# Attention steps in another order: values ahead of transposes on TensorE, copies between two exponentials on ScalarE

## The reference, cut to what matters

```python
s = jnp.einsum('bhqd,bhrqwd->bhqrw', q_i, k_win).astype(jnp.float32)
s = s + jnp.transpose(bias, (0, 2, 1, 3)).astype(jnp.float32)[None]
pr = jax.nn.softmax(s.reshape(B, H, GRID_W, kh * kw), axis=-1).reshape(B, H, GRID_W, kh, kw)
return jnp.einsum('bhqrw,bhrqwd->bhqd', pr.astype(v.dtype), v_win)
```

```python
o_dil = dilated_attention(q_d, k_d, v_d, positions, slopes).reshape(B, S, -1).astype(x.dtype)
o_mla = latent_attention(cq, ckv, k_rope, positions, g_cq[l], w_q_up[l], g_ckv[l], w_kv_up[l], ...)
mix = jnp.concatenate([o_dil, o_mla], axis=-1) @ w_out[l]
```

## Time and profile before

| | before |
|---|---|
| median of 3 runs | 3013.02 us (3012.51 to 3015.49) |
| the profiled execution: its time | 3010.71 us |
| its span, first to last instruction | 3008.9 us |
| PE busy | 2906.1 us (97% of the span) |
| DVE busy | 1765.0 us (59%) |
| ACT busy | 1313.7 us (44%) |

### The profile page before, as it was taken

How to read it: one execution, slowest core, us unless ns; L and a number is a source line. 1 busy time by engine, 2 the same in 40 slices (tenths; PEclk the granted TensorE clock), 3 DMA queues, 4 the chain that set the end, 5 groups by cost and what they waited for, 6 DMA issues and landing times. The chain is left out here.

```text
span 3008.9 us, 47845 instructions
## 1 busy us (share of the span) xinstructions
PE 2906.1 (97%) x20088; PEld 2310.8 (77%) x20088; DVE 1765.0 (59%) x2421; ACT 1313.7 (44%) x2015; POOL 214.7 (7%) x353
## 2 busy tenths in 40 slices
PE   8999888999999999999999999999999999999999
PEld 6756777888888786788888875688888865788887
DVE  5357775696864767487784577553333586543332
ACT  4234443442434537443334546654152556553241
POOL 0400000100000111000000212000000212000000
PEclk9999999999999999999999999999999999999999
DMA  5310001556523231365643220023222310123222
GB/s 168 98 62 3 4 3 58 147 176 226 173 86 105 78 111 65 88 203 197 188 130 102 89 86 1 30 86 102 94 96 96 96 60 2 58 85 100 95 98 84
DMA packets 224165, 287.97 MB, mean 96 GB/s; under 512 B 8031, under 2 KB 164103, under 8 KB 217808
## 3 DMA queue, kind: packets, MB, share of 16 engines
q1 hardware_dynamic: 213632, 226.32, 23.8%
q0 software_dynamic: 8448, 54.34, 5.3%
q10 hardware_dynamic: 1872, 4.26, 0.4%
HBM read 280.70 MB, written 2.10 MB: 94 GB/s over the span
## 5 line engine op out<-in xcount | busy, mean ns | idle before, releaser
L240 DVE TENSOR_TENSOR weights_operand<-weights,weights_operand 128x2048 fp32r<-128x2048 f32 x196 | 448.8, 2290 | 450.2 <-ACT weights_operand L234 439.7
L234 ACT CAST weights_operand<-weights 128x2048 fp32r<-128x2048 f32 x196 | 374.0, 1908 | 511.9 <-PE ps L248 505.4
L246 PE MATMUL ps<-ffn_h_high,weights_operand 128*128 128x512 f32 x704 | 274.5, 390 | 2.2 <-PEq L507 2.2
L248 PE MATMUL ps<-ffn_h_high,weights_operand 128*128 128x512 f32 x704 | 273.9, 389 | 0.0
L247 PE MATMUL ps<-ffn_h_low,weights_operand 128*128 128x512 f32 x704 | 273.9, 389 | 0.0
L246 PE MATMUL ps<-mlp_h_high,weights_operand 128*128 128x512 f32 x512 | 200.3, 391 | 2.5 <-DVE mlp_h_low L828 2.1
L248 PE MATMUL ps<-mlp_h_high,weights_operand 128*128 128x512 f32 x512 | 199.3, 389 | 0.0
L247 PE MATMUL ps<-mlp_h_low,weights_operand 128*128 128x512 f32 x512 | 199.2, 389 | 0.0
L246 PE MATMUL ps<-weights_operand,mlp_hid_high 128*128 128x512 f32 x512 | 199.2, 389 | 0.0
L247 PE MATMUL ps<-weights_operand,mlp_hid_high 128*128 128x512 f32 x512 | 199.2, 389 | 0.0
L248 PE MATMUL ps<-weights_operand,mlp_hid_low 128*128 128x512 f32 x512 | 199.2, 389 | 0.0
(11 more groups left out here) (582 smaller groups left out, 6171.9 us busy)
## 6 DMA issues: line engine op xcount, KB each, us to landing
mod_w<-in_w_mod POOLq DMA_DIRECT2D x48, 1024.0 KB, 5.2
weights<-in_ffn_w_up SPq DMA_DIRECT2D x88, 512.0 KB, 5.2
weights<-in_w_mlp_in SPq DMA_DIRECT2D x32, 1024.0 KB, 5.3
weights<-in_w_mlp_out SPq DMA_DIRECT2D x32, 1024.0 KB, 5.0
weights<-in_ffn_w_down SPq DMA_DIRECT2D x24, 768.0 KB, 4.4
weights<-in_mix_w_in SPq DMA_DIRECT2D x13, 1024.0 KB, 5.3
weights<-in_na_w_qkv SPq DMA_DIRECT2D x12, 1024.0 KB, 5.1
weights<-in_w_in SPq DMA_DIRECT2D x12, 1024.0 KB, 5.4
```

What stands on the lines that cost most here:

```text
L234: nc.scalar.copy(st.high[s][:], st.raw[s][:]).then_inc(st.high_done, 1)
L240: nc.vector.tensor_tensor(st.low[s][:], st.raw[s][:], st.high[s][:], ALU.subtract).then_inc(st.split_done, 1)
L246: nc.tensor.matmul(out, lh, rh, start=start, stop=False)
L248: return nc.tensor.matmul(out, ll, rh, start=False, stop=stop)
```

## The change

Two lists are written in another order; no instruction is added or taken away, and every instruction keeps its waits. On PE the spread and values of unit s-2 stand ahead of the transposes of unit s-1 instead of behind them. On ACT the two copies of unit s-1 stand between the first and the second exponential of unit s instead of ahead of both. DVE's and POOL's lists stay. All five calls are concerned.

```diff
@@ tensor
-                    if 0 <= s - 1 < N:
-                        u = s - 1
-                        for h in range(2):
-                            pe.wait_ge(U.exp, 2 * u + h + 1)
-                            if u:
-                                pe.wait_ge(U.copied, 2 * u - 1 + h)
-                            for n in range(slots):
-                                mm = nc.tensor.transpose(ps[:, 4 + h, n * P:(n + 1) * P], S[u % 2][h][:, n * P:(n + 1) * P],
-                                                         cx.ident[:])
-                            mm.then_inc(U.turned, 1)
                     if 0 <= s - 2 < N:
                         u = s - 2
                         pe.wait_ge(U.widened, u + 1)
...
                         mm.then_inc(U.out, 1)
+                    if 0 <= s - 1 < N:
+                        u = s - 1
+                        for h in range(2):
+                            pe.wait_ge(U.exp, 2 * u + h + 1)
...
+                            mm.then_inc(U.turned, 1)
@@ scalar
+                def copy(u):
+                    for h in range(2):
+                        act.wait_ge(U.turned, 2 * u + h + 1)
...
+                def exponential(s, h):
...
                 for s in range(N + 2):
+                    if s < N:
+                        exponential(s, 0)
                     if 0 <= s - 1 < N:
...
+                        copy(s - 1)
                     if s < N:
...
+                        exponential(s, 1)
```

More of the change, by code:

```diff
@@ L3047, in _ @@
                         mm.then_inc(U.out, 1)
+                    if 0 <= s - 1 < N:
+                        u = s - 1
+                        for h in range(2):
+                            pe.wait_ge(U.exp, 2 * u + h + 1)
+                            if u:
+                                pe.wait_ge(U.copied, 2 * u - 1 + h)
+                            for n in range(slots):
+                                mm = nc.tensor.transpose(ps[:, 4 + h, n * P:(n + 1) * P], S[u % 2][h][:, n * P:(n + 1) * P],
+                                                         cx.ident[:])
+                            mm.then_inc(U.turned, 1)
             @block.scalar
@@ L3052, in _ @@
                     first[0](act)
+                def copy(u):
+                    for h in range(2):
+                        act.wait_ge(U.turned, 2 * u + h + 1)
+                        if u >= 2:
+                            act.wait_ge(U.out, u - 1)
+                        nc.scalar.copy(PT[u % 2][h][:], ps[:, 4 + h, 0:width].rearrange("p (a q) -> p a q", a=slots))\
+                            .then_inc(U.copied, 1)
+                def exponential(s, h):
+                    m = M[s % 2]
+                    act.wait_ge(U.best, 2 * s + h + 1)
+                    if s >= 2:
+                        act.wait_ge(U.turned, 2 * (s - 2) + h + 1)
+                        act.wait_ge(U.inverted, s - 1)
+                    src = S[s % 2][h][:] if score_op else ps[:, bank(s, h), :]
+                    nc.scalar.activation(S[s % 2][h][:], src, ACT.Exp, scale=exp_sign, bias=m[:, 2 + h:3 + h],
+                                         accum_out=m[:, 4 + h:5 + h]).then_inc(U.exp, 1)
                 for s in range(N + 2):
+                    if s < N:
+                        exponential(s, 0)
                     if 0 <= s - 1 < N:
[L3055 to L3061, removed]
-                    if s < N:
[L3063 to L3071, removed]
+                        copy(s - 1)
+                    if s < N:
+                        exponential(s, 1)
             @block.vector
```

## The result

| | before | after |
|---|---|---|
| median | 3013.02 us (3012.51 to 3020.93, 5 runs) | 3026.53 us (3023.53 to 3030.81, 5 runs) |
| the profiled execution: its time | 3010.71 us | 3024.65 us |
| first scores of `naa` to the end of the span | 1874.0 us | 1883.9 us |

The ratio of the times is 1.0036, with a 95% interval of 1.0023 to 1.0049: slower by 10.8 us (6.9 to 14.8), while the two medians, of five runs each, lie 13.5 apart. The sign is as forecast; the median lies 1.0 above the top of the range given, and the time that the ratio gives, 3023.9, inside it.

The account below looks back on a forecast made before the run. PE was busy 97% of the span; a loop through three engines set `naa`, DVE bounded `dia`, PE `mla`. Terms 3.3 + 4.7 - 0.9 = +7.1 us on the median 3013.0 gave 3020.1, range 3014 to 3025.5.

Parts of the forecast that it names:

- the multiplication's loop: In `dia`, spread waits for the previous unit's multiplication, transposes now between: 7.00 us per two steps, 3.50 against 3.32; +4.7 both calls.
- the copies' loop: In `naa`, values wait for copies behind the first exponential: 4.43 us per two steps, 0.11 more a step, +3.3 us.
- Ends of calls: At call ends, last spread's shorter wait and last exponential's place behind two copies taken as equal: 0.
- `mla`: In `mla`, PE bounds and nothing new waits: minus 0.10 plus 0.07, -0.03 us a step; thirty steps, -0.9.
- The loops have slack: Rival for `naa` and `dia`: unseen slack in the loops, so little happens, 3012.1 us; chance 0.35.
- The waits for the exponential go and nothing takes their place: Rival: in `naa` PE does values during its 0.33 wait, step falls to 2.00; in all -9.1 us, 3003.9; chance 0.05.
- Changes of shape: On PE in `naa` and `dia`, four changes of array shape a step instead of three: 0.09 us more.

## Why the prediction came out as it did

- **`dia`, the multiplication's loop: right.** 7.00 was worked out for two steps, 7.00 measured (3.37 + 3.63), with the wait where it was looked for. Opening and steady steps give +2.3 in `dia0`, the term as predicted. That ScalarE has no part in it is shown by PE's half alone (3.50), that the spread closes it by the spread put late (3.32).
- **`naa`, the copies' loop: the size of a step right, the mechanism half the story.** 0.11 a step was predicted; 0.11 was measured over 12 steps, 0.13 over the 25 of the table (3.15 in all). But "before, the copies ... were no part" left out that the multiplication's loop, worked out for `dia` alone, also closes in `naa`: in the kernel with PE's half alone it is 0.79 from scores to score operation (1186.25), 1.57 to the multiplication (1187.82), 0.53 to the spread, 0.23 to the values, 0.59 to the transposes and 0.59 to the next scores, 4.30 for two steps. PE's order by itself so costs about 0.05 a step and the copies' place another 0.06. That the step still came out at nearly the size given is partly luck: the loop left out is the shorter one, 4.30 against the 4.39 of the copies' loop (4.43 predicted).
- **The opening of `naa`: mis-sized.** The prediction counted its five steps like all others, 0.6 us. It cost 2.2: 1.2 at equal clock, and 1.0 more because half clock lasted 10.2 us in place of 6.8. In the three executions of each kernel the opening's mean clock was 0.77, 0.77, 0.87 before and 0.69, 0.78, 0.69 after. The other kernels without fillers had 0.59 (PE's half alone), 0.88 (ACT's half alone), 0.76 and 0.77 (spread late). That the new order's pauses prolong half clock fits this, but so few executions do not show it; that it is absent with two matmuls more in the opening is shown by the traces of the three kernels that have them (mean clock 1.00 in each, one execution each).
- **"Ends of calls: I take these as equal: 0" failed.** In `dia0` the last values now wait 0.71 for copies that start only when the last transposes, moved to the end of their step, are done, and the spread ahead of those transposes waits 1.29 for its multiplication; before, the last spread waited 0.49. In all PE stands 2.33 from the last scores on (9.32 less 6.99 busy), where it stood 1.70. Last scores to last multiplication went from 8.87 to 9.32 in `dia0`, and from 8.87 to 9.21 in `mla0` (scores at 1934.94 and 1945.12). Four calls of that kind make +1.6.
- **`mla`: right in kind.** A step went from 3.92 to 3.88, -0.04 where -0.03 was predicted; what its end took back leaves -0.3 a call, -0.6 for both instead of -0.9.
- **The sum.** `naa` +5.1, `dia0` +2.8, `dia1` +3.7, `mla` -0.6: +11.0 against +7.1. Of the 3.9 missing, 1.6 is the ends of four calls. Another 1.9 is half clock of which the first execution of the kernel before had less: 1.0 in `naa`'s opening, and 0.9 in `dia1`, which took 58.72 there at a mean clock of 1.00, but 59.64 in the second execution, at 0.97, and 62.44 at 0.97 in the changed kernel. The small rest is the work of `naa`'s opening and 0.4 of its steady steps, less what its end and `mla`'s steps gave back.
- **The rivals.** "The loops have slack" falls: both close, as rows show. "The waits for the exponential go and nothing takes their place" falls for this change, but its place was real: with the spread late and the copies ahead, `naa` runs at 1.96, under the 2.00 that it named.
- **Changes of shape: right in kind, priced too low.** Four a step in place of three were priced at 0.09 more. A step in which PE has no stop went from 2.00 to 2.14 in `naa` (1182.51 to 1184.65; 2.13 with PE's half alone, 1179.09 to 1181.22, where the copies are early), and from 3.21 (1800.72 to 1803.93) to 3.37 (1808.86 to 1812.23) in `dia0`. So the fourth change cost 0.13 to 0.16: 0.08 to 0.09 at the transposes, the rest at the spread, which is now itself the first matmul behind the scores and is followed by the values after 0.26 instead of 0.20, a term that the prediction left out. PE's own 3.37 is more than the 3.32 of VectorE, so about 0.05 of the 0.18 a step in `dia` would be there without the multiplication's loop, and the loop adds the other 0.13.

## What to carry to other kernels

Before two blocks of one engine's list are swapped, follow every wait that now stands ahead of a longer block: here the spread, one matmul of 0.20 us with a wait for VectorE's last multiplication, was moved in front of the transposes, and so put another 1.0 us of TensorE's work (in `dia`) into a loop that had room for 0.7 before VectorE has to wait for it. Sum such a loop over all engines in every stage where the list is used, not only in the one where it looks tightest, and price filling and emptying apart from the steady steps. Where times scatter by more than the effect, measure in the trace from the first instruction that differs.

## What the runs showed of the hardware that was not expected

- Ahead of the first changed instruction the same instructions took from 1134.9 to 1143.1 us in 13 executions, while from there to the end the kernel before repeated within 2.4 us and the changed one within 0.7, in three executions each. The unchanged work between `naa` and `dia0` took from 578.4 to 581.8.
- The granted clock at the opening of `naa` differed between executions of the same program, behind the same work (mean 0.77, 0.77 and 0.87 in the kernel before). Two filler matmuls between the second scores and the first transposes, where PE paused for 1.55 us in the first execution of the kernel before, kept it at 1.00 in three kernels, one execution each.
